# Twenty gate and up products of two feed-forward layers, each done as a 2x2 block product with seven multiplications instead of eight

## The reference, cut to what matters

```python
def swiglu(x, wi, wo):
    gate, up = jnp.split(x @ wi, 2, axis=-1)          # wi: 1024 x (2 * 2816)
    return (jax.nn.silu(gate) * up) @ wo
h = h + 0.5 * swiglu(rms_norm(h, ffn1_norm[li]), ffn1_wi[li], ffn1_wo[li])
```

## Time and profile before

| | us |
|---|---|
| median of 3 runs (2770.95 to 2773.82) | 2772.65 |
| the profiled execution | 2773.5 |
| its span, first to last instruction | 2771.8 |

### The profile page before, as it was taken

One profiled execution on the slowest core, in us unless ns is written; L12 is line 12 of the kernel. 1 busy time (PEld: TensorE's weight loads), 2 busy tenths in 40 slices (PEclk: granted clock), 3 DMA queues, 4 the chain that ended last, 5 costly groups with the idle time before them and its releaser, 6 DMA issues.

```text
span 2771.8 us, 39060 instructions
## 1 busy us (share of the span) xinstructions
PE 2718.9 (98%) x14176; PEld 2210.0 (80%) x14176; DVE 1577.0 (57%) x2453; ACT 1205.8 (44%) x1814; POOL 624.0 (23%) x607
## 2 busy tenths in 40 slices
PE   8999999999999999999899999999999999899998
PEld 6888888788888888887778888877888888777777
DVE  5444336544443575435865764338777777676664
ACT  4333232443322333223553333236655555457775
POOL 3000013100001451003733530014322222123232
PEclk9999999999999999999999999999999999999999
DMA  5333332233333564333203653322222222122222
GB/s 151 93 97 93 99 83 77 84 91 98 98 92 98 144 185 134 93 97 84 84 12 110 189 159 95 99 74 77 69 69 69 69 69 69 43 74 64 68 61 69
DMA packets 484826, 255.23 MB, mean 92 GB/s; under 512 B 17843, under 2 KB 478422, under 8 KB 484710
## 3 DMA queue, kind: packets, MB, share of 16 engines
q1 hardware_dynamic: 484534, 253.40, 31.9%
q10 hardware_dynamic: 176, 0.27, 0.0%
HBM read 251.51 MB, written 2.13 MB: 92 GB/s over the span
## 4 chain that ended last, share of the span: by engine, by line
PE 91%; DVE 6%; ACT 1%; POOL 1%; issue 1%; DMA 0%; SPq 0%; DVEq 0%; POOLq 0%; ACTq 0%
PE bank L259 73%; PE bank L1881 2%; PE bank L1912 1%; PE bank L1914 1%; PE bank L1913 1%; DVE dsa_work L1578 1%; DVE w_lo L245 1%; DVE small L1572 1%; PE bank L1988 1%; PE bank L2796 1%; PE bank L2788 1%; PE bank L2025 1%; PE bank L2821 1%; DVE gdn_blocks L2385 1%; PE bank L981 1%
## 5 line engine op out<-in xcount | busy, mean ns | idle before, releaser
L259 PE MATMUL bank<-x_hi,w_hi 128*128 128x512 f32 x2320 | 936.6, 404 | 8.6 <-DVE w_lo L245 4.8
L259 PE MATMUL bank<-x_hi,w_lo 128*128 128x512 f32 x2320 | 907.6, 391 | 0.0
L259 PE MATMUL bank<-x_lo,w_hi 128*128 128x512 f32 x2320 | 906.7, 391 | 0.6 <-DVE x_lo L586 0.6
L245 DVE TENSOR_TENSOR w_lo<-w_raw,w_hi 128x1024 fp32r<-128x1024 f32 x429 | 531.0, 1239 | 556.3 <-ACT w_hi L239 555.7
L239 ACT ACTIVATE w_hi<-w_raw 128x1024 fp32r<-128x1024 f32 x429 | 450.6, 1055 | 621.4 <-PE bank L259 572.1
L259 PEld LDWEIGHTS bank<-x_hi,w_hi 128*128 128x128 f32 x2320 | 437.1, 188 | 106.5 <-issue 16.1
L259 PEld LDWEIGHTS bank<-x_hi,w_lo 128*128 128x128 f32 x2320 | 436.2, 188 | 93.2
L259 PEld LDWEIGHTS bank<-x_lo,w_hi 128*128 128x128 f32 x2320 | 437.5, 189 | 87.5 <-issue 3.6
L435 POOL TENSOR_TENSOR sumsq<-sumsq,sq 128x512 f32<-128x512 f32 x56 | 92.3, 1648 | 1293.0 <-ACT sq L421 1292.4
L259 PE MATMUL bank<-h_hi,w_hi 128*128 128x512 f32 x768 | 298.9, 389 | 1.6 <-DVE h_lo L1612 1.6
L259 PE MATMUL bank<-h_hi,w_lo 128*128 128x512 f32 x768 | 298.8, 389 | 0.0
(11 more groups left out here) (486 smaller groups left out, 3474.9 us busy)
## 6 DMA issues: line engine op xcount, KB each, us to landing
w_raw<-in_ffn_wi_dram SPq DMA_DIRECT2D x176, 512.0 KB, 3.8
w_raw<-in_ffn_wo_dram SPq DMA_DIRECT2D x64, 512.0 KB, 4.1
w_raw<-in_ada_w_dram SPq DMA_DIRECT2D x48, 512.0 KB, 4.9
w_raw<-in_a_w_in_dram SPq DMA_DIRECT2D x48, 512.0 KB, 4.0
w_raw<-in_b_w_in_dram SPq DMA_DIRECT2D x32, 512.0 KB, 4.2
w_raw<-in_ffn_wo_dram SPq DMA_DIRECT2D x32, 384.0 KB, 3.5
w_raw<-in_even_w_in_dram SPq DMA_DIRECT2D x16, 512.0 KB, 4.0
w_raw<-in_a_w_out_dram SPq DMA_DIRECT2D x16, 512.0 KB, 3.4
```

The lines of the kernel that those rows point to most:

```text
L245: dve.tensor_tensor(w_lo[s][:], w_raw[raw_of(b) % RAW][:], w_hi[s][:].bitcast(F32), ALU.subtract).then_inc(w_lo_done, 1)
L259: mm = pe.matmul(out, lhs[:, w], rhs(kt), start=first and kk == 0 and m == 0, stop=last and kk == len(kts) - 1 and m == 2)
```

## The change

In ffn0 and ffn1, pairs 4 to 13 (ten of 22, `SEVEN_AT, SEVEN_N = 4, 10`) are no longer two blocks of eight row tiles. The weights of a pair are taken as a 2x2 matrix (gate or up; first or second half of the 1024 rows), x as another (first or second half of the rows; tokens 0 to 255 or 256 to 511), and their product is formed with seven block products and sums before and after. A block product is a group of 12 matmuls (4 row tiles times three) over 256 columns (`seven_group`); a pair has 84 of them.

- **x sums**: ACT writes x_part = gain times `hres` (8 instructions of 128x512, in the layer's first two pairs), GpSimd forms four sums of 128x1024, ACT and DVE split each into hi and lo. Once per layer.
- **Weight sums**, per pair: GpSimd adds `w_both` (128x512) and a second one (`three_pool`, 128x512, over the gate block's left half). Two more are made by DMAs that GpSimd issues and that add into their destination, 256 KB each: `low_pool` into the up block's left half, `all_pool` into `w_all`, a single buffer that SP fills anew for each pair with another 256 KB load (`all_sp`).
- **Splits**, per pair: ACT makes hi parts of left, both and all (512 columns each) and of row and low (1024 each), DVE the lo parts. Before there were two of 1024.
- **Evacuation**, per pair: ACT copies P1 to the other bank and P7 to SBUF (256 columns each), DVE has six instructions over 256 columns and the product and `h_lo` over 512.
- **Order**: each engine gets a hand-written order for the ten pairs. For pair n (turn n), cut to its core:

```diff
 SP
+                for n in range(SEVEN_N + 2):
+                    if 2 <= n <= SEVEN_N:
+                        all_sp(sp, f, n - 1, lambda m: src(m, n - 1))
+                    seven_sp(sp, f, n, src)
+                    if n == 0:
+                        all_sp(sp, f, 0, src)
+        def all_sp(sp, f, n, src):
+            if n:
+                sp.wait_ge(all_lo, seven(f) + n)
+            sp.dma_start(w_all[:, :]..., src(0)[:, KT // 2:KT, :]).then_inc(*by_dma(all_loaded, f, n))
+        def seven_sp(sp, f, n, src):
+            for m in range(2):
+                if n >= 2:
+                    if m == 0:
+                        sp.wait_ge(*of_dma(all_sum, f, n - 2))
+                        sp.wait_ge(row_lo, c + 1)
+                    else:
+                        sp.wait_ge(low_lo, c + 1)
...
+                sp.dma_start(dst, src(m)).then_inc(w_loaded[(raw + m) % RAW], 16)
 PE
+            for n in range(SEVEN_N):
+                pe.wait_ge(row_lo, c + 1)
+                pe.wait_ge(p1_copied, c + 1)
+                seven_group(pe, slot_of(f, 0), 0, part_pair(2), B[:, T1])
+                pe.wait_ge(p7_copied, c + 1)
+                seven_group(pe, slot_of(f, 0), 1, own_pair(1, T1), A[:, T1]).then_inc(p2_done, 1)
+                if n:
+                    last_pe(pe, f, n - 1)          # waits all_lo, last_joined, tile_free; then p3_done
+                if n + 1 < SEVEN_N:
+                    first_and_seventh_pe(pe, f, n + 1, 1)   # waits left_lo
+                    first_and_seventh_pe(pe, f, n + 1, 7)   # waits both_lo; then p7_done
+                pe.wait_ge(low_lo, c + 1)
+                pe.wait_ge(p7_joined, c + 1)
+                seven_group(pe, slot_of(f, 3), 0, part_pair(1), B[:, T1])
+                seven_group(pe, slot_of(f, 3), 1, part_pair(3), B[:, T2]).then_inc(p4_done, 1)
 ACT
+            for n in range(SEVEN_N):
+                if n + 1 < SEVEN_N:
+                    row_act(act, f, n + 1)         # waits three_added, p2_done
...
+                all_act(act, f, n)                 # waits all_sum, p3_done of pair n - 1
+                if n:
+                    seven_silu(act, f, n - 1)
+                if n + 2 < SEVEN_N:
+                    left_act(act, f, n + 2)        # waits the load of the gate block n + 2
+                if n + 1 < SEVEN_N:
+                    copy_act(act, f, n + 1)        # waits p7_done; then p1_copied, p7_copied
+                if n:
+                    seven_h_hi(act, f, n - 1)
+                if n + 1 < SEVEN_N:
+                    low_act(act, f, n + 1)         # waits low_sum
+                if n + 2 < SEVEN_N:
+                    both_act(act, f, n + 2)
 DVE
+            for n in range(SEVEN_N):
+                if n:
+                    last_dve(dve, f, n - 1)
+                low_dve(dve, f, n)
+                if n and n + 1 < SEVEN_N:
+                    both_dve(dve, f, n + 1)
+                join_dve(dve, f, n)
+                if n + 1 < SEVEN_N:
+                    row_dve(dve, f, n + 1)
...
+                if n:
+                    gate_dve(dve, f, n - 1)
+                all_dve(dve, f, n)
+                if n:
+                    up_dve(dve, f, n - 1)
+                    product_dve(dve, f, n - 1)
+                if n + 2 < SEVEN_N:
+                    left_dve(dve, f, n + 2)
+                if n:
+                    h_lo_dve(dve, f, n - 1)
 POOL
+            for n in range(SEVEN_N - 1):
+                all_pool(pool, f, n + 1)           # waits all_loaded; DMA with accumulation
+                if n + 2 < SEVEN_N:
+                    both_pool(pool, f, n + 2)      # waits both raw blocks of pair n + 2
+                    three_pool(pool, f, n + 2)     # waits left_lo
+                    low_pool(pool, f, n + 2)       # DMA with accumulation
```

More of the change, by code:

```diff
@@ L44 @@
 OUT3 = 3
+SEVEN = (0, 1)
+SEVEN_AT, SEVEN_N = 4, 10
+HT = T // 2
 FFN_B, FFN_T = 2 * FT + OUT3 * KT, 2 * FT + KT
@@ L198, in first_and_second_block @@
         ada_made, ada_added, ada_summed = sem("ada_made"), sem("ada_added"), sem("ada_summed")
+        part_made, part_added, part_hi, part_lo = sem("part_made"), sem("part_added"), sem("part_hi"), sem("part_lo")
+        left_hi, both_hi, row_hi, low_hi, all_hi = (sem(f"{n}_hi") for n in ("left", "both", "row", "low", "all"))
+        left_lo, both_lo, row_lo, low_lo, all_lo = (sem(f"{n}_lo") for n in ("left", "both", "row", "low", "all"))
+        both_added, three_added = (sem(f"{n}_added") for n in ("both", "three"))
+        p1_done, p7_done, p2_done, p3_done, p4_done = (sem(f"p{n}_done") for n in (1, 7, 2, 3, 4))
+        p1_copied, p7_copied, p7_joined, first_taken, last_joined, up_scaled = (
+            sem(n) for n in ("p1_copied", "p7_copied", "p7_joined", "first_taken", "last_joined", "up_scaled"))
+        low_sum, all_sum, all_loaded = ([sem(f"{n}{k}") for k in range(2)] for n in ("low_sum", "all_sum", "all_loaded"))
         normed = sem("normed")
@@ L735, in ffn_act @@
             split_hi(act, b0 + AHEAD)
-            ffn_turns(act, f, turn)
+            if f in SEVEN:
+                for k in range(SEVEN_AT // 2 - 1):
+                    turn(4 * k, 4, k, 0, False)
+                seven_act(act, f)
+                k = (SEVEN_AT + SEVEN_N) // 2
+                with act.Fori(0, FT // 2 - k) as i:
+                    turn(4 * k, 4, k, i, False)
+            else:
+                ffn_turns(act, f, turn)
             down_act(act, b0 + 2 * FT, FT, after, 1)
@@ L764, in turn @@
                     dve.tensor_tensor(h_lo[:, h], prod[s][:], h_hi[:, h].bitcast(F32), ALU.subtract).then_inc(h_ready, 1)
-            ffn_turns(dve, f, turn)
+            if f in SEVEN:
+                for k in range(SEVEN_AT // 2 - 1):
+                    turn(4 * k, 4, k, 0, False)
+                seven_dve(dve, f)
+                k = (SEVEN_AT + SEVEN_N) // 2
+                with dve.Fori(0, FT // 2 - k) as i:
+                    turn(4 * k, 4, k, i, False)
+            else:
+                ffn_turns(dve, f, turn)
             if ada_of(f):
@@ new lines, in seven_group, with part_pair @@
+        def seven_group(pe, slot, h, x, out, first=False):
+            hi, lo = w_hi[slot], w_lo[slot]
+            x_h, x_l = x
+            for k in range(4):
+                w = slice(h * T + k * P, h * T + k * P + P)
+                for m, (lhs, rhs) in enumerate(((hi, x_h), (hi, x_l), (lo, x_h))):
+                    mm = pe.matmul(out, lhs[:, w], rhs[:, k, :], start=first and k == 0 and m == 0, stop=k == 3 and m == 2, skip_group_check=True)
+            return mm
+        def part_pair(m):
+            return fourths(t_hi[m]), fourths(t_lo[m])
@@ new lines, in left_act, with both_act @@
+        def left_act(act, f, n):
+            b = seven_block(f, n)
+            act.wait_ge(*loaded(raw_of(b)))
+            if n:
+                act.wait_ge(p1_done, seven(f) + n)
+            else:
+                act.wait_ge(block_done, b - 3 + SPLIT + 1)
+            act.activation(w_hi[slot_of(f, 1)][:, RIGHT_H], w_raw[raw_of(b) % RAW][:, LEFT_H], ACT.Copy).then_inc(left_hi, 1)
+        def both_act(act, f, n):
+            c = seven(f) + n
+            act.wait_ge(both_added, c + 1)
+            if n:
+                act.wait_ge(p7_done, c)
+            else:
+                act.wait_ge(block_done, seven_block(f, 0) - 2 + SPLIT + 1)
+            act.activation(w_hi[slot_of(f, 2)][:, LEFT_H], w_both[:], ACT.Copy).then_inc(both_hi, 1)
@@ new lines, in row_act, with low_act @@
+        def row_act(act, f, n):
+            c, b = seven(f) + n, seven_block(f, n)
+            act.wait_ge(three_added, c + 1)
+            if n:
+                act.wait_ge(p2_done, c)
+            else:
+                act.wait_ge(block_done, b - 4 + SPLIT + 1)
+            act.activation(w_hi[slot_of(f, 0)][:], w_raw[raw_of(b) % RAW][:], ACT.Copy).then_inc(row_hi, 1)
+        def low_act(act, f, n):
+            c, b = seven(f) + n, seven_block(f, n)
+            act.wait_ge(*of_dma(low_sum, f, n))
+            if n:
+                act.wait_ge(p4_done, c)
+            else:
+                act.wait_ge(block_done, b - 1 + SPLIT + 1)
+            act.activation(w_hi[slot_of(f, 3)][:], w_raw[(raw_of(b) + 1) % RAW][:], ACT.Copy).then_inc(low_hi, 1)
@@ new lines, in all_act, with copy_act @@
+        def all_act(act, f, n):
+            c = seven(f) + n
+            act.wait_ge(*of_dma(all_sum, f, n))
+            if n:
+                act.wait_ge(p3_done, c)
+            act.activation(w_hi[slot_of(f, 1)][:, LEFT_H], w_all[:], ACT.Copy).then_inc(all_hi, 1)
+        def copy_act(act, f, n):
+            A, B = seven_banks(f, n)
+            act.wait_ge(p7_done, seven(f) + n + 1)
+            act.wait_ge(tile_free, seven_tile(f, n) + 2)
+            act.activation(B[:, T1], A[:, T1], ACT.Copy).then_inc(p1_copied, 1)
+            if n >= 2:
+                act.wait_ge(last_joined, seven(f) + n - 1)
```

(21 more changed lines are left out.)

297 lines of the change are left out of this document (293 added, 4 removed).

## The result

The changed kernel takes 2836.83 us (median of 4 runs, 2836.08 to 2837.03), the kernel before 2772.32 in the same comparison: ratio 1.0232, 95% interval 1.0217 to 1.0246. The profiled execution took 2836.66 us, span 2834.9, against 2773.5 and 2771.8. Forecast were 2838 us, in a range of 2788 to 2890.

A forecast was written before the change was run, and what follows sets the result against it. PE bound the kernel before; after the change a chain of waits would gate eight of ten turns. 2773.5 plus 62.8 for two layers plus 2 for ways in and out gave 2838 us, range 2788 to 2890.

The forecast's parts named there:

- The four waits: Ten pairs: copy behind left, left on its load, load behind `all_sp`, all lo on P3, chaining each gated turn.
- The length of a turn: Gated turns, eight of ten a layer: 14.1 us each, 14.95 with the mean clock loss.
- The floor of 11.5: Gated turn: shortest chain of three PE groups, splits, `w_all` issue, gate block DMA, left and copy, 11.5 us.
- PE's idle time ahead of the copy: Eight of ten turns: PE idle 3 to 6 us in one piece ahead of the first group.
- From the turn's start to all lo: Gated turn: late up block, two GpSimd sums, row hi, row lo, gate and all lo, ending at 8.0 us.
- From all lo to the next turn: Gated turn: SP hand-over and issue 0.14 and 0.37, landing 4.35, left, copy and hand-overs 1.28 us.
- The clock: 0.85 a turn: Gated turns: granted clock falls after PE's idle time, losing 1.7 us in half of them, 0.85 on the mean.
- The matmul of 256 columns: PE in the ten pairs: one start every 0.115 us, weight load just hidden, 9.66 us a pair.
- rival in which PE sets the pace: Ten pairs: gate block in time, copy never late, a turn is seven groups; 2751 us, chance 0.07.
- The sum: Ten pairs: 15 groups 20.7 us plus eight turns of 14.95, 140.3 against 108.9, +31.4 a layer, +62.8 for two.
- ways in and out: Into and out of the ten pairs: 1 us added a layer, taken between 0 and 3.
- Accumulating DMAs: GpSimd-issued adding DMAs: up to 8.6 us beyond a plain 2.9 us costs nothing; nothing charged.

The follow-up runs named there:

- two_w_all: Changed kernel with a second buffer for `w_all`, so SP's load waits for all lo of two pairs back: 2765.11 us, 0.9973 to the kernel before.
- small_sums: Changed kernel with GpSimd's two weight sums cut to 8 of 512 columns from each layer's second pair on: 2830.68 us, 1.0206 to the kernel before.
- early_load: Changed kernel with SP issuing a pair's two block loads ahead of the `w_all` load of the pair before: 2805.19 us, 1.0120 to the kernel before.
- early_pool: Changed kernel with block loads ahead of `w_all` on SP and GpSimd's sum of both blocks ahead of the accumulating DMA: 2797.01 us.

## Why the prediction was right, and which terms were off

*The four waits.* Right, and the point that decided. Eight waits a layer for the copy, SP behind all lo, the load, left, copy. two_w_all takes out one of them and the whole loss goes with it.

*The length of a turn.* Expected 14.1, with the clock 14.95; measured 14.26 (89.20 to 189.00, seven turns) and 14.44 (649.15 to 750.24), mean 14.35. The floor of 11.5 was kept by all. PE's idle time ahead of the copy, forecast at 3 to 6 us, was under 3 in nine of the sixteen (2.1 to 5.1), since its own work was longer: wider spacing, and a slow clock in twelve.

*From the turn's start to all lo: 8.0 expected.* 8.0 measured (160.65 to 168.70). I had it through the late up block, two sums, row hi and row lo. That path is there, and nearly as I laid it out: the first sum starts 0.93 into the turn (1.14 forecast), the second ends at 4.75 (4.2), row hi at 5.85 (5.5). But a second path is as long, one that I hadn't laid end to end: DVE's in-order queue, with seven operations ahead of row lo that I had counted in DVE's 8.4 us by sum only. The timelines of GpSimd, ACT and DVE in the changed kernel:

```profile
163.32 2.08 POOL L1272 TENSOR_TENSOR w_raw<-w_both,w_raw 128x512 f32<-128x512 f32 x1
165.44 1.06 ACT L1025 ACTIVATE w_hi<-w_raw 128x1024 fp32r<-128x1024 f32 x1 [1.60 <-POOL w_raw L1272]
166.22 0.41 DVE L1162 TENSOR_TENSOR gate_s<-bank,rstd 128x256 f32<-128x256 f32 x1
```

Row hi ends at 166.50, DVE comes free for row lo at 166.63. In ten of the fourteen turns counted (seven a layer) the two are within 0.13 us of each other, DVE last; in three row hi waits for PE's second group, slow by the clock, and ends last; in one it is 1.3 us ahead. That the path I had left out was no longer than the one I had is luck. small_sums shows the third path, PE's.

*From all lo to the next turn: 6.1 expected* (0.14 and 0.37, 4.35, 1.28), 6.0 measured (168.70 to 174.73), with 4.09 and 4.30 for the DMA.

*The clock: 0.85 a turn.* Mis-sized, and in the wrong place. The clock did fall, in more turns than the half I assumed: it was 0.50 to 0.67 in the first 4.3 us of twelve of the sixteen turns behind a wait for the copy, as in the first of these windows over two turns of the changed kernel (0.61 in the first 4.25 us of one, 1.00 in the same part of the next):

```profile
160.65:164.90 4.25, 4.25 (x23) 4.25 (x24) 3.86 (x6) 2.24 (x4) 3.18 (x2) 0.61 0.30 54
174.73:179.00 4.27, 4.27 (x36) 4.27 (x37) 3.88 (x6) 2.25 (x4) 2.93 (x2) 1.00 0.30 56
```

23 matmuls were done at the one and 36 at the other, and the turns took 14.08 and 14.27 us. While PE works slowly the others run the same path (DVE 3.86 and 3.88 us busy), and PE's delay only eats its own idle time. In the fourteen turns counted, the way from copy to the end of all lo takes 8.50 to 8.58 us in the four at 1.00, 8.25 to 8.57 in the eight at 0.60 to 0.67, and 8.97 and 9.25 in the two at 0.50. So inside the gated turns the clock cost about 1 us in all. I charged a slower PE to a loop in which PE was hardly a link.

It cost more where PE is the chain, and there I had charged nothing: in turn 8, which waits for one last copy and has no load behind it. The chain of waits:

```profile
189.00 20.00 PE bank L936 x144
750.24 19.00 PE bank L936 x144
```

144 matmuls at 0.120 are 17.28 us, so 2.7 and 1.7 us are lost. Behind the 4.1 us wait for L1124 in the first layer, 12 matmuls took 2.90 us (1.44 at 0.120) and the next 12, of 512 columns, 4.27 (2.72 at the 0.2268 of the earlier trace rows): another 3.0, at a granted clock of 0.50 and then 0.63. In all the clock took about 8.4 us, against the 13.6 forecast for the turns.

*The matmul of 256 columns: 0.115 expected.* 0.120, as the timeline of PE shows in a stretch at full clock (changed kernel, start us, us in flight, what):

```profile
194.80 0.29 PE L936 MATMUL bank<-x_hi,w_hi 128*128 128x256 f32 x1
194.92 0.28 PE L936 MATMUL bank<-x_lo,w_hi 128*128 128x256 f32 x1
```

The weight load adds little if anything, and a pair is 84 x 0.120 = 10.08 us, not 9.66. The most that the change can save is 20 x 0.81 = 16.2 us instead of 24.6. The rival in which PE sets the pace would so have been 2759, and two_w_all, which comes nearest to that rival, shows 2765 (it keeps the waits on the way in). The Trainium skill (TensorE: Matmul & The Clock Gate, Back-to-back issue gap) has 262 cycles for 256 columns, 0.109 at 2.4 GHz, for an isolated one, and says that in a stream with weight loads both set the spacing. The row lies 0.011 over the first figure, as the second sentence would have it; that the weight load is the reason no run here shows.

*The sum.* 15 groups of 1.44 and eight turns of 14.35 give 136.4 a layer, +27.5 over the 108.9 of the earlier trace rows, 55.0 for two. The 64.6 measured leave 9.6 for ways in and out where I had 2. 4.1 of that is PE's wait for L1124 in the first layer, DVE behind contended operations, and 3.0 the slow matmuls behind it; 0.7 its wait for L1130 on the way in to the second; 4.4 the clock in turn 8. Together 12.2. Against that stands turn 0 of each layer, counted above at 14.35: it took 12.3 (76.93 to 89.20) and 13.2 (636.00 to 649.15), 3.3 less for the two. That leaves 8.9, and 0.7 that I haven't placed. So the turns were 9.6 too long (16 x 0.60), the 30 other groups 1.8 too short (0.06 each) and the ways in and out 7.6 too short: errors that cancel, and a time that is nearer (2838 against 2837) than its terms.

*Accumulating DMAs: nothing up to 8.6 us.* Right. The issues of the stretch (count, KB each, median us to landing):

```profile
w_all<-w_raw POOLq DMA_DIRECT2D x8, 256.0 KB, 4.2
w_raw<-w_raw POOLq DMA_DIRECT2D x7, 256.0 KB, 3.3
```

PE shows no wait for low or all in the changed kernel. It took early_load and early_pool to put one of them on the path.

## What to carry to other kernels

Before trusting sums of busy time, write down for each wait what stands ahead of it in its own queue, and follow the loop once round: if a buffer has one copy and its refill stands in the same queue as the loads with lead, the lead is gone. When PE waits, the named releaser is only the last link; reordering moves the gap to another engine (three orders here gave turns of about 14.1, 12.4 and 12.0 us on the mean, each over another loop), while one more buffer removed the loop. A slower clock costs nothing while the engine has slack in the loop, and its full price in the turns where the engine is the chain; so price it turn by turn. Before pricing contention, lay the rival paths beside each other: the gain from shortening one ends at the length of the next.

## What the runs showed that I had not expected

- A 256-column float32 matmul with its own weights starts every 0.120 us, 0.005 more than two neighbouring ones in another place of the same kernel; over 1680 matmuls that is 8 us.
- A DVE subtraction of 1024 columns (1.21 us alone) took 3.42 us, and a product of 512 columns 2.88 instead of 0.69, while GpSimd summed 1024 columns for 2.4 to 3.4 us. For the product the added time is three times the operation's own length.
- An accumulating DMA of 256 KB between two places in SBUF lands in 3.3 to 4.2 us (median) with loads beside it, and GpSimd is held about 0.9 us by its issue.
- The granted clock fell after idle times of 2 to 5 us as well, in one turn and not in the next with the same idle time (2.15 ahead of 160.65, 2.33 ahead of 174.73; 3.35 ahead of 722.01 at 1.00, 3.31 ahead of 735.97 at 0.66), so which turns it will hit couldn't be told from the idle time.
